# Alternating the products A12·B21 and A11·B11 of a feed-forward pair between two PSUM banks

## The reference, cut to what matters

```python
D_FF = int(math.ceil(8 * D_MODEL / 3 / 256) * 256)      # 2816
def _swiglu(h, w_gate, w_up, w_down):
    g = h @ w_gate.astype(h.dtype)
    u = h @ w_up.astype(h.dtype)
    return (jax.nn.silu(g) * u) @ w_down.astype(h.dtype)
```

## Time and profile before

| | us |
|---|---|
| median of 3 runs (1879.77 to 1882.09) | 1880.53 |
| the profiled execution's own time | 1881.34 |
| its span in the trace | 1879.7 |
| PE busy | 1855.0 (99%) |
| DVE busy | 1280.9 (68%) |
| ACT busy | 942.7 (50%) |
| matmuls of lines 738 to 740, in all four parts | 3696 |

### The profile page before, as it was taken

How to read it: one execution, slowest core, us unless ns; L and a number is a source line. 1 busy time by engine, 2 the same in 40 slices (tenths; PEclk the granted TensorE clock), 3 DMA queues, 4 the chain that set the end, 5 groups by cost and what they waited for, 6 DMA issues and landing times.

```text
span 1879.7 us, 30172 instructions
## 1 busy us (share of the span) xinstructions
PE 1855.0 (99%) x10662; PEld 1554.9 (83%) x10662; DVE 1280.9 (68%) x2220; ACT 942.7 (50%) x1573; POOL 233.2 (12%) x322
## 2 busy tenths in 40 slices
PE   9999999999999999999999999999999999999998
PEld 7787899889987777789989998776777887777777
DVE  7787888548865767788846876576667565666553
ACT  6576566325544444556523654355554344445442
POOL 3111011001000000011001100000002063532000
PEclk9999999999999999999999999999999999999999
DMA  7334476357422222267545742211323233323221
GB/s 252 110 101 124 129 197 175 104 145 192 130 93 79 59 65 67 84 151 185 135 145 142 193 127 73 72 46 58 96 68 92 75 94 81 91 79 94 74 100 63
DMA packets 79219, 208.64 MB, mean 111 GB/s; under 512 B 10208, under 2 KB 18528, under 8 KB 79120
## 3 DMA queue, kind: packets, MB, share of 16 engines
q1 hardware_dynamic: 60080, 174.16, 29.0%
q0 software_dynamic: 19040, 33.20, 10.4%
HBM read 203.12 MB, written 4.21 MB: 110 GB/s over the span
## 4 chain that ended last, share of the span: by engine, by line
PE 90%; DVE 4%; DMA 3%; ACT 1%; issue 1%; SPq 0%; POOL 0%; DVEq 0%; ACTq 0%
PE ps L652 17%; PE ps L654 16%; PE ps L653 16%; PE ps L738 4%; PE ps L739 4%; PE ps L740 4%; PE ps L943 3%; PE tr L909 3%; PE sc L738 3%; PE sc L739 3%; PE sc L740 3%; PE sc L866 2%; PE sc L652 1%; PE sc L653 1%; PE sc L654 1%; DMA scr<-in_w 1%
## 5 line engine op out<-in xcount | busy, mean ns | idle before, releaser
L652 PE MATMUL ps<-Hl,Wh 128*128 128x512 f32 x784 | 328.4, 419 | 0.0
L1353 ACT ACTIVATE Wh<-Wr 128x1024 fp32r<-128x1024 f32 (+2 forms) x172 | 195.7, 1139 | 257.3 <-PE ps L654 230.7
L654 PE MATMUL ps<-Hh,Wh 128*128 128x512 f32 x784 | 307.2, 392 | 0.0
L653 PE MATMUL ps<-Hh,Wl 128*128 128x512 f32 x784 | 306.4, 391 | 0.0
L1937 DVE TENSOR_TENSOR Wl<-Wr,Wh 128x1024 fp32r<-128x1024 f32 (+2 forms) x172 | 231.5, 1346 | 104.8 <-ACT Wh L1353 103.4
L652 PE MATMUL ps<-Yl,Wh 128*128 128x512 f32 (+1 forms) x648 | 251.9, 389 | 0.8 <-DVE Yl L1986 0.8
L653 PE MATMUL ps<-Yh,Wl 128*128 128x512 f32 (+1 forms) x648 | 248.9, 384 | 0.0
L654 PE MATMUL ps<-Yh,Wh 128*128 128x512 f32 (+1 forms) x648 | 248.9, 384 | 0.0
L652 PEld LDWEIGHTS ps<-Hl,Wh 128*128 128x128 f32 x784 | 147.4, 188 | 40.2 <-issue 11.1
L654 PEld LDWEIGHTS ps<-Hh,Wh 128*128 128x128 f32 x784 | 147.2, 188 | 32.9
L653 PEld LDWEIGHTS ps<-Hh,Wl 128*128 128x128 f32 x784 | 147.8, 189 | 25.7 <-issue 0.5
(11 more groups left out here) (418 smaller groups left out, 4151.8 us busy)
## 6 DMA issues: line engine op xcount, KB each, us to landing
Wr<-in_w SPq DMA_DIRECT2D x162, 512.0 KB, 3.6
Wr<-in_w SPq DMA_DIRECT2D x30, 768.0 KB, 4.2
scr<-in_w SPq DMA_DIRECT2D x66, 256.0 KB, 4.7
Wr<-in_w SPq DMA_DIRECT2D x66, 256.0 KB, 4.6
scr<-in_w SPq DMA_DIRECT2D x22, 512.0 KB, 5.3
scr<-in_w POOLq DMA_DIRECT2D x44, 256.0 KB, 7.4
Wr<-in_w POOLq DMA_DIRECT2D x44, 256.0 KB, 4.2
Wr<-in_w SPq DMA_DIRECT2D x14, 640.0 KB, 3.8
```

The source lines that it names most:

```text
L652: pe.matmul(bank[:, 0:n], hi, rl[:, k, :], start=(k == 0), stop=False)
L653: pe.matmul(bank[:, 0:n], lo, rh[:, k, :], start=False, stop=False)
L654: return pe.matmul(bank[:, 0:n], hi, rh[:, k, :], start=False, stop=(k == kc - 1))
L1353: act.activation(place(Wh, slot, kc), place(Wr, slot, kc), ACT.Copy).then_inc(w_hi, 1)
```

## The change

The two products A12·B21 and A11·B11 are no longer issued one behind the other, but matmul by matmul in turn, one into `beta_` (bank `ps[2 + par]`), one into `alpha` (bank `ps[par]`). A new helper issues the 24 matmuls. `p2_ok` is given by the last matmul of A12·B21, which is now the 23rd of the 24, and `w_used` by the 24th as before. The wait for `e_ok` (in the second pair of a part with a normalisation ahead: for `x_ok`) that stood between the two products now stands ahead of both.

```diff
+                def first_two(alpha, beta_):
+
+                    for j in range(4):
+                        th, tl = quarter("B21", j)
+                        uh, ul = quarter("B11", j)
+                        at, cs = slice(S + j * P, S + (j + 1) * P), slice(j * P, (j + 1) * P)
+                        for w, t, u, first, last in ((Wh, tl, ul, j == 0, False), (Wl, th, uh, False, False),
+                                                     (Wh, th, uh, False, j == 3)):
+                            mm = pe.matmul(beta_, w[:, 0, at], t, start=False, stop=last, skip_group_check=True)
+                            if last:
+                                mm.then_inc(p2_ok, 1)
+                            mm = pe.matmul(alpha, w[:, 0, cs], u, start=first, stop=last, skip_group_check=True)
+                    mm.then_inc(w_used, 1)
+
...
                     pe.wait_ge(w_lo, b + lo_at["A"])
-                    product("A12", "B21", beta_).then_inc(p2_ok, 1)
                     if not one:
                         pe.wait_ge(e_ok, 4 * g + (4 * p0 - 2))
                     elif ready:
                         pe.wait_ge(x_ok, X0[AFTER[ready]] + 8)
-                    product("A11", "B11", alpha, True).then_inc(w_used, 1)
+                    first_two(alpha, beta_)
```

## The result

The changed kernel took 1892.28 us (median of 4 runs, 1891.20 to 1894.16) against 1880.16 of the kernel before in the same comparison (4 runs): a ratio of 1.0063, with a 95% interval from 1.0046 to 1.0081. That is 12.1 us slower; 1893.0 was forecast. The profiled execution took 1894.16, its span is 1892.5 against 1879.7.

A forecast was written before the change was run, and what follows sets the result against it. PE was taken as the bound (90% of the chain that ended last). 28 pairs at 0.33 (9.2) plus 4 at 0.80 (3.2) give 12.4, say 12.5, over the 1880.53 median: 1893.0 us; range 1886 to 1899.

The forecast's parts named there:

- The pace of the matmuls: The 24 reordered matmuls per pair: alternating banks costed at nothing; bounds 0.32 us a pair saved to 0.12 lost.
- The rival of cheaper matmuls: Alternating banks saves up to 13 ns per matmul, 0.32 us a pair; about 1882.5 us; chance 0.07, 0.03 of it faster.
- the rival of 5 ns more: Each alternated matmul costs 5 ns more, 4.8 us in all, giving 1898; chance 0.07.
- the rival that ACT and DVE make up the lateness: Loop pairs hide the 1.32 us before S2·T2; only last pairs pay, 1883.7 us; chance 0.05.
- The wait that moves ahead: Wait for `e_ok`, 1.44 us earlier, before A12·B21: costs nothing, as its signal comes 0.8 us before; `x_ok` nothing either.
- The late signal: `p2_ok` 1.32 us later delays ACT's copy, then S2·T2 through `Yh` and `Yl`: PE waits 0.24, price 0.33 a pair.
- The four pairs before the last: Not priced apart: among the 28 pairs at 0.33 us, with S4·B22 taken as covered by 0.2.
- The last pairs: Last pair of each part: A22·T4 waits directly for the copy, 0.71 late plus 0.09; 0.80 us each, four pairs.
- The pairs that don't pay: Four second pairs (no `Yh`, `Yl`) pay nothing; four early pairs with late loads lose 0.1 us at most.
- the loads: Rival: SP's loads, issued behind S1's low part, become late too; some 0.25 us a pair more, 1900; chance 0.10.
- The sum: 28 pairs at 0.33 plus 4 last pairs at 0.80: 12.4 us, say 12.5; bounds 8.8 and 14.

The follow-up runs named there:

- the second experiment: Kernel before with only the wait for e_ok (x_ok in the second pair) moved ahead of A12·B21: 1881.29 us against 1879.64, ratio 1.0011.

## Why the prediction was right

- **The pace of the matmuls: right.** Costed at nothing; 0.12 within banks and across them, and 36 alternating pairs at the old length once the two waits are covered. The rival of cheaper matmuls falls with it, and the rival of 5 ns more as well; the rival that ACT and DVE make up the lateness falls with the 10.40 of the loop pairs. The Trainium skill (TensorE: Matmul & The Clock Gate, "Wait — 56ns, not 53.3ns?") gives about 2.5 ns over the columns; here 13 ns stand over them in one bank and in two, so whatever the other 11 are, the bank is not it.
- **The wait that moves ahead: right.** Nothing, by the second experiment.
- **The late signal: right in the loop.** The copy was forecast 4.40 after the pair's start and came 4.39; S2·T2 was forecast 0.24 late and came 0.22 late; 0.33 a pair was forecast and measured, in 24 pairs. (The prediction says that DVE's 59.78 of 70.47 counts overlaps twice; a busy time counts them once. Nothing in the sum rests on it.)
- **The four pairs before the last: wrong in the path, by a tenth of a microsecond each.** They were counted with the loop pairs and paid 0.23. There the chain from copy to S2·T2 is 2.83 (500.81 to 503.63), so S2·T2 comes only 0.03 late. But it leaves S4·B22, 1.44 behind it, to wait as well: the third read ends at 505.05 (504.63 + 0.42), S4·B22 starts at 505.20, and that is 0.15 behind its predecessor instead of 0.12. The prediction called S4·B22 covered by 0.2, but counted to the end of the read and left out the 0.15 between it and the matmul, although its own chain has 0.14 in such a place. Two waits of 0.03, and 0.10 and 0.07 for PE to get going again, make the 0.23.

```profile
500.81 0.60 ACT L1517 ACTIVATE rstd<-sc 128x512 f32<-128x512 f32 x1 [2.06 <-PE sc L751]
```

```profile
504.63 0.42 DVE L2165 TENSOR_TENSOR gs<-ps,acc 128x256 f32<-128x256 f32 x1
```

```profile
503.48 0.28 PE L740 MATMUL sc<-Eh,Wh 128*128 128x256 f32 x1
503.63 0.39 PE L738 MATMUL ps<-El,Wh 128*128 128x256 f32 x1
503.86 0.28 PE L739 MATMUL ps<-Eh,Wl 128*128 128x256 f32 x1
...
505.05 0.28 PE L740 MATMUL ps<-Eh,Wh 128*128 128x256 f32 x1
505.20 0.36 PE L738 MATMUL ps<-Hl,Wh 128*128 128x256 f32 x1
505.39 0.28 PE L739 MATMUL ps<-Hh,Wl 128*128 128x256 f32 x1
```

- **The last pairs: right in kind, small by a tenth.** Forecast 0.80, measured 0.89. The mis-sized term is the 0.63 from the copy's start to A22·T4, taken from the earlier trace rows; here it is 0.74 (511.10 to 511.84), and it is 0.74 in all four last pairs. In these traces it is 0.63 wherever a late load had held the copy up. The trace of before had a longer one too: 0.72 in the first pair of a part (222.29 to 223.01). What makes the difference is open.

```profile
511.10 0.60 ACT L1517 ACTIVATE acc<-sc 128x512 f32<-128x512 f32 x1 [2.98 <-PE sc L751]
```

```profile
511.84 0.36 PE L738 MATMUL sc<-El,Wh 128*128 128x256 f32 x1 [0.66 <-ACT acc L1517]
```

- **The pairs that don't pay, and the loads: not refuted, and not shown.** The second pairs and the four late early pairs moved by -0.8 to +1.1 us and by +0.5 in all, as much as they do under edits that leave their loads alone, so "0.1 at most" cannot be read from one execution. The loop pairs show no sign of late loads: all 24 are between 10.39 and 10.41.
- **The sum: right, partly by chance.** 12.4 was forecast; the pairs give 7.9 + 0.9 + 3.6 = 12.4, since the error of the last pairs (+0.4) and that of the pairs before the last (-0.4) cancel.

The Trainium skill (Perfetto Trace Analysis, "Matmuls") would have groups rotate through banks so that the evacuation of one lies under the next. The runs agree, and add what decides: not the banks but the time at which the first group ends, since the late signal in the old order of matmuls cost the same.

## What to carry to other kernels

When two accumulation groups are interleaved, both end when the last one ends; cost the change by the consumer of the group that used to end first, and follow that consumer's queue, because what is lost may be two instructions further back in it. A pair in the old trace that was late for another reason is the best price list there is: one such pair gave 0.31 us, and 24 pairs paid 0.33. Before an engine's signal is moved, find the instant from which lateness reaches the bound engine (here 4.17 us into a loop pair and 3.57 into a last one, both worked out from the chains); up to it the move is free.

## What the runs showed of the hardware that was not expected

A wait of PE costs more than its length: the second matmul behind it comes 0.22 or 0.19 behind the first instead of 0.12, and this stood even behind the waits of 0.03 in the pairs before the last.

The granted clock fell to half, the 1.2 GHz level, behind some waits of PE and not behind others that were as long. In the first pair of the third part no matmul started from 815.22 to 817.23 before the change, and none from 822.88 to 824.90 after it, 2.0 us in both. The two pairs, before and after:

```profile
813.00:822.48 9.48, 7.45 (x50) 7.07 (x48) 6.38 (x10) 4.05 (x7) 0.87 (x1) 0.82 0.23 35
```

```profile
820.66:828.65 7.99, 5.97 (x50) 5.58 (x48) 6.39 (x10) 4.06 (x7) 0.87 (x1) 1.00 0.31 54
```

In the kernel with the last pairs alone alternated, PE started no matmul from 245.38 to 248.10, 2.7 us, and stayed at full speed. In the kernel with the copy ahead of S3, a shorter wait, from 246.25 to 248.42, was followed by steps of 0.21 instead of 0.12, and by a clock of 0.53:

```profile
248.90:252.40 3.50, 3.50 (x19) 3.50 (x18) 2.73 (x6) 0.29 (x1) 0.00 (x0) 0.53 0.92 253
```

So a stall of 2 to 3 us can cost about another 1.5 us, 16 matmuls at 0.21 instead of 0.12, or nothing; the length of the stall alone did not tell which. Within the four parts, the traces of before and after have it in first pairs alone (in two before, in one after), so it is no part of the 13.0 us of the 40 pairs, but it takes 1.5 us off the difference of the two spans.
